# Cached values of seven batches spread over eight pairs, the eighth beside the output projection; prompt scores in split q and k

## The chip, the cores and the metric

One NeuronCore of a Trainium2 chip runs the whole program. The metric is the device time in microseconds (us) of one execution. Before the change it is 1991.42 us, the median of three runs (1989.58 to 1993.14).

## What is computed

A two-layer decoder step for a prompt group (one sequence of 1024 tokens) and a sample group (eight sequences of four new tokens, each with 4096 cached positions in 32 pages of 128). The first layer is a pooling mixer, the second "forgetting attention" with 16 heads of width 64. Only the second layer and its output projection matter here:

```python
def fox_attend(q, cq, qpos, k, ck, kpos, v):     # prompt and sample alike
    s = einsum('bqhd,bkhd->bhqk', q, k) * scale
    s = s + cq[..., :, None] - ck[:, None, :]     # forget values, cumulated
    s = where(kpos <= qpos, s, -inf)
    return einsum('bhqk,bkhd->bqhd', softmax(s), v)

y = (o * silu(z)) @ w_out                         # both groups
x = x + y;  y_out = rms_norm(x, final_norm)
```

For the sample group, k and v are the pages that a page table names, followed by the four new rows. All pages of the cached values are 134 MB in float32.

## The kernel before, in words

The attention phase comes after the projection phase. The sample scores (q times cached k) have already been computed there and lie in DRAM as `s_scr`. What is left runs as a loop over eight **pairs** (`pair(b)`, one on each engine). Pair `b` does two things at once: the whole prompt attention of heads 2b and 2b+1, and the softmax and values of sample batch `b` (all 16 heads).

A pair has eight **slots**, one for each block of 128 prompt queries, in the order `QBLOCKS = (0, 7, 1, 6, 2, 5, 3, 4)`. Slot `s` needs scores against 128 to 1024 keys for two heads. TensorE (PE) computes them in plain float32 (`scores`, line 1519: `qa` and `ka`, 66 rows, two of them for the forget values; a float32 matmul shows as two records) into `ps_a` and `ps_c`. VectorE (DVE) takes the maximum (`prompt_max`, L1800), ScalarE (ACT) the exponential (`prompt_exp`, L1702), DVE multiplies by the reciprocal of the sum (`prompt_norm`, L1805 and L1808), PE transposes (`prompt_turn`, L1547), ACT copies out (`prompt_evac`, L1709), and PE multiplies with the values in the next slot (`prompt_values`, L1560). DVE then gates the result (`gate`, L1869).

Between these steps PE takes cached value pages of the sample batch (`sample_pages`, L1592; eight records for a page). `V_FIRST` spreads the 32 pages of a batch over the slots as 2, 6, 2, 6, 3, 5, 4, 4. For every eight pages (an octet `o`) there is one `sample_scores(b + 1, o)` on DVE (L1826, L1830, for the following batch), one `sample_exp` on ACT (L1717), one `sample_turn` on PE (L1572) and one `sample_evac` on ACT (L1727). `new_scores`, `common_max`, `new_turn`, `sample_last`, `sum_exp` and `sample_out` come once for each batch.

Every engine runs its instructions in the written order. SyncE (SP) issues the loads in the order of the pages: `v_page(b, p)` waits until the page that was in one of the ring's `VR = 8` places has been used, then loads 512 KB. Into that stream are written the loads of the next pair's q and k rows (`qk_rows`), its prompt values (`v_pair`), and two `score_half` (each 512 KB of `s_in` and twice 256 KB of `d_sb`, the decay terms) for each batch. A load written late therefore waits behind the pages ahead of it.

Before pair 0, DVE does all four `sample_scores(0, o)`, `new_scores(0)` and `common_max(0)`; pair 0's `prompt_max` stands behind them.

After pair 7 comes the output projection over eight row tiles (L1665 to L1667): z and w_out are split into a high and a low part in `float32r` (ACT makes the high part, L1747 and L1751; DVE subtracts for the low part, L1893 and L1899), and each product is three passes (high·high, high·low, low·high). The sample rows are projected in between, and each tile is normalised and stored. The same three-pass form is used in all projections (L812 to L814).

Of the kernel before, what the change touches and what calls it, by code (L numbers as in the profile page):

```python
# [26 lines left out]
P = 128  # L27
# [89 lines left out]
def build(nc, x_prompt, x_sample, state_pool, cache_k, cache_v, cache_logf, page_table, norm_g,  # L117
# [17 lines left out]
    with ExitStack() as ctx:  # L135
# [130 lines left out]
        ka = [place(f"ka{i}", [AUG, 2, SEQ], F32, big_at(at_qk[i] + 2048)) for i in range(2)]  # L266
        v_pr = [place(f"v_pr{i}", [P, TT, P], F32, big_at((AT_F + 4096, 15168)[i])) for i in range(2)]
# [6 lines left out]
        wo_at = [big_at(n) for n in (9024, 10048, 0, 1024, 4160, 5184, 6208, 7232)]  # L274
# [5 lines left out]
        fn_b = place("fn_b", [P, DM], F32, big_at(AT_K + 2048))  # L280
# [58 lines left out]
        ld_v_first, ld_qk_first = sem("ld_v_first"), sem("ld_qk_first")  # L339
# [21 lines left out]
        def v_pair(eng, b):  # L361

            eng.dma_start(v_pr[b % 2][:, :, :], v_prompt[0, 0].rearrange("(t p) h d -> p t (h d)", p=P)
                          [:, :, P * b:P * b + P]).then_inc(ld_v[b % 2] if b else ld_v_first, 16)

        def qk_rows(eng, b, i):
# [3 lines left out]
                .then_inc(ld_qk[b % 2] if b else ld_qk_first, 16)  # L370
# [996 lines left out]
        T2 = [("s", 0)]  # L1367
        for s_ in range(SLOTS):
            T2 += [(h_, s_, f_) for h_ in range(2) for f_ in range(len(fills(s_, h_)))]
            if s_ in (1, 3, 5):  # L1370
                T2.append(("s", (s_ + 1) // 2))
            if s_ == 5:
                T2.append(("n",))

        def t2_name(key):
            return "z" if key[0] == "s" else "x" if key[0] == "n" else fills(key[1], key[0])[key[2]][2]
# [4 lines left out]
        def t2_at(b, key):  # L1381

            return b * len(T2) + T2.index(key)

        def t2_free(b, key):

            i = b * len(T2) + T2.index(key)
            same = [j for j in range(i) if t2_name(T2[j % len(T2)]) == t2_name(key)]
# [3 lines left out]
        V_FIRST = (0, 2, 8, 10, 16, 19, 24, 28, 32)  # L1392
        W_ORDER = (4, 5, 6, 7, 0, 1, 2, 3)

        w_full = [sem(f"w_full{k}") for k in range(KT8)]
        ld_os, ld_fn, st_o, st_y, o_free = (sem(n) for n in ("ld_os", "ld_fn", "st_o", "st_y", "o_free"))
# [9 lines left out]

        act_wh, dve_wl, act_zh, dve_zl = (sem(n) for n in ("act_wh", "dve_wl", "act_zh", "dve_zl"))
# [3 lines left out]
        def sync_attend(sp):  # L1411
# [14 lines left out]
            def next_pair(b, p):  # L1426

                if p == VR + 2 and b < NB - 1:
                    sp.wait_ge(pe_s, 16 * b) if b else sp.wait_ge(pe_qk, UNITS)
                    qk_rows(sp, b + 1, 0)  # L1430
                if p == VR + 5 and b < NB - 1:
                    qk_rows(sp, b + 1, 1)
                if p == VR + 8 and b < NB - 1:
                    past(sp, pe_pvp, SLOTS * b)
                    v_pair(sp, b + 1)
# [7 lines left out]
            for b in range(NB - 1):  # L1443
                for p in range(VR, PAGES):
                    v_page(b + 1, p)
                    next_pair(b, p)
                for p in range(VR):
                    v_page(b + 2, p)
            for k in range(4, KT8):
                w_out_rows(k)  # L1450
            for p in range(VR, PAGES):
                v_page(NB, p)
                if p == 15:
                    sp.wait_ge(pe_s, 16 * (NB - 1))
                    for k in range(4):
                        w_out_rows(k)
            sp.wait_ge(st_y, 16 * (TT + 1))

        def gpsimd_attend(pool):
# [32 lines left out]
            pool.wait_ge(pe_pv, VR + PAGES * NB)  # L1492
# [14 lines left out]
        def tensor_attend(pe):  # L1507
# [16 lines left out]
            def new_scores(b):  # L1524
# [3 lines left out]
                if b:  # L1528
                    pe.wait_ge(act_t2, t2_at(b - 1, (1, 6, 0)) + 1)
# [497 lines left out]
```

## Time and profile before

| what | us |
|---|---|
| median of three runs | 1991.42 |
| profiled execution, its time | 1999.29 |
| profiled execution, its span | 1997.6 |
| attention, pairs 0 to 7 (1353 to 1887) | 534 |
| of it pair 0, from its first score (1353 to 1444) | 91 |
| output projection and end (1887 to 1998) | 111 |

In the page, PE is busy for 92% of the span and the DMA engines carry 207 GB/s on average. How to read the stages: the window view gives busy time, instruction count, the clock granted to TensorE (as a share of 2.4 GHz), the mean busy share of the 16 DMA engines, and GB/s, for each stretch. The timeline gives the start of each group of instructions and, in brackets, the engine's idle time before it and what ended that.

### The profile page before, as it was taken

What the parts mean: (1) busy time and instruction counts of PE and PEld (TensorE: products, weight loads), DVE (VectorE), ACT (ScalarE), POOL (GpSimd) and SP (SyncE); (2) the same over time, 40 slices, a digit from 0 to 9 for tenths busy, and PEclk for the clock granted to TensorE, in tenths of its full rate; (3) what the DMA queues carried; (4) which work ended last, traced back from release to release, by engine and by line L of the source; (5) the groups of instructions that cost most, each with busy time, mean ns of one, the idle gap of its engine ahead of it and who ended that gap; (6) DMA issues with size and microseconds to landing.
All of it is one profiled execution on the core that took longest, in us unless ns stands there. A gap on an engine that the chain in (4) does not pass through costs nothing.

```text
span 1997.6 us, 37941 instructions
## 1 busy us (share of the span) xinstructions
PE 1837.1 (92%) x15120; PEld 1362.1 (68%) x15120; DVE 1124.7 (56%) x1810; ACT 547.3 (27%) x1241; POOL 296.4 (15%) x328
## 2 busy tenths in 40 slices
PE   4999999999999989899989999885999998999997
PEld 3877887787788767677778777773545554555676
DVE  5434544474465367877776777663545554554533
ACT  5121121121111143111112111212444444454521
POOL 0000000000000003444444444330000000000100
PEclk9999999999999989899999999996899999999999
DMA  5111111111112156899999999989999899999721
GB/s 139 38 45 53 43 45 42 48 43 49 43 48 64 32 177 231 286 339 313 319 319 351 321 323 308 329 296 333 336 330 305 301 333 327 311 327 344 271 85 56
DMA packets 228677, 414.49 MB, mean 207 GB/s; under 512 B 17553, under 2 KB 137010, under 8 KB 228238
## 3 DMA queue, kind: packets, MB, share of 16 engines
q1 hardware_dynamic: 168364, 252.17, 38.0%
q0 software_dynamic: 42160, 150.54, 21.2%
q10 hardware_dynamic: 17986, 9.42, 1.7%
q8 instruction: 121, 1.98, 0.4%
q14 instruction: 46, 0.38, 0.1%
HBM read 370.85 MB, written 41.94 MB: 207 GB/s over the span
## 4 chain that ended last, share of the span: by engine, by line
PE 52%; DMA 22%; DVE 13%; SPq 5%; issue 4%; POOL 2%; ACT 2%; POOLq 0%; DVEq 0%; ACTq 0%
DMA k_raw<-in_cache_k_dram,k_idx 16%; PE ps_a L812 5%; PE ps_a L814 4%; PE ps_a L813 4%; DVE kt L1293 4%; PE ps_b L812 3%; PE ps_b L814 3%; PE ps_b L813 3%; PE ps_c L812 3%; DMA d_sb<-decay 3%; PE ps_b L1592 3%; PE ps_c L814 3%; PE ps_c L813 3%; SPq L359 3%; PE ps_b L1560 2%
## 5 line engine op out<-in xcount | busy, mean ns | idle before, releaser
L1293 DVE STREAM_TRANSPOSE kt<-k_raw 128x1024 f32<-128x1024 f32 x256 | 309.9, 1232 | 145.7 <-DMA k_raw<-in_cache_k_dram,k_idx 140.6
L353 POOL DMA_INDIRECT k_raw<-in_cache_k_dram,k_idx x256 | 256.3, 1001 | 449.2 <-DVE kt L1293 291.0
L812 PE MATMUL ps_a<-h_hi,w_hi 128*128 128x512 f32 x656 | 263.2, 401 | 3.2 <-DVE w_lo L1115 3.2
L814 PE MATMUL ps_a<-h_hi,w_lo 128*128 128x512 f32 x656 | 256.4, 391 | 0.0
L813 PE MATMUL ps_a<-h_lo,w_hi 128*128 128x512 f32 x656 | 256.4, 391 | 0.0
L1115 DVE TENSOR_TENSOR w_lo<-w_raw,w_hi 128x1024 fp32r<-128x1024 f32 x97 | 109.1, 1125 | 163.1 <-ACT w_hi L642 160.4
L1592 PE MATMUL ps_b<-v_pg,pt_s 128*16 128x256 f32 x2048 | 147.4, 400 | 17.2 <-DMA v_pg<-in_cache_v_dram 16.1
L812 PE MATMUL ps_b<-h_hi,w_hi 128*128 128x512 f32 x384 | 154.2, 401 | 2.7 <-DVE w_lo L1115 2.7
L812 PEld LDWEIGHTS ps_a<-h_hi,w_hi 128*128 128x128 f32 x656 | 123.5, 188 | 39.1 <-issue 10.8
L814 PE MATMUL ps_b<-h_hi,w_lo 128*128 128x512 f32 x384 | 150.0, 391 | 0.0
L813 PE MATMUL ps_b<-h_lo,w_hi 128*128 128x512 f32 x384 | 149.7, 390 | 0.0
L954 PE MATMUL ps_c<-kt,q_bd 128*32 128x128 f32 x4096 | 136.4, 290 | 11.0 <-DVE kt L1293 9.8
L814 PEld LDWEIGHTS ps_a<-h_hi,w_lo 128*128 128x128 f32 x656 | 123.5, 188 | 26.6
L813 PEld LDWEIGHTS ps_a<-h_lo,w_hi 128*128 128x128 f32 x656 | 123.8, 189 | 23.8
L954 PEld LDWEIGHTS ps_c<-kt,q_bd 128*32 128x32 f32 x4096 | 117.5, 117 | 26.6 <-issue 23.3
L1800 DVE TENSOR_REDUCE pp_nm<-ps_a 128x1 f32<-128x128 f32 (+3 forms) x64 | 48.4, 756 | 151.5 <-PE ps_a L1521 151.3
L1173 DVE TENSOR_TENSOR x_p<-x_p,ps_c 128x512 f32<-128x512 f32 x128 | 87.6, 687 | 78.0 <-PE ps_c L814 78.0
L642 ACT CAST w_hi<-w_raw 128x1024 fp32r<-128x1024 f32 x97 | 96.0, 989 | 120.0 <-PE ps_c L814 86.3
L812 PE MATMUL ps_c<-w_hi,y_hi 128*128 128x512 f32 x256 | 103.9, 406 | 2.8 <-DVE x_p L1173 2.7
L814 PE MATMUL ps_c<-w_hi,y_lo 128*128 128x512 f32 x256 | 101.7, 397 | 0.0
L813 PE MATMUL ps_c<-w_lo,y_hi 128*128 128x512 f32 x256 | 101.7, 397 | 0.0
L1709 ACT COPY pt_p<-b 128x384 f32<-128x384 f32 (+3 forms) x168 | 73.6, 468 | 97.8 <-PE b L1547 96.1
(284 smaller groups left out, 2854.5 us busy)
## 6 DMA issues: line engine op xcount, KB each, us to landing
v_pg<-in_cache_v_dram SPq DMA_DIRECT2D x256, 512.0 KB, 7.6
w_raw<-in_w_in_pool_dram SPq DMA_DIRECT2D x32, 512.0 KB
w_raw<-in_w_in_attn_dram SPq DMA_DIRECT2D x32, 512.0 KB
w_raw<-in_w_out_pool_dram SPq DMA_DIRECT2D x16, 512.0 KB
s_scr<-ss_st ACTq DMA_DIRECT2D x64, 128.0 KB, 6.2
s_in<-s_scr SPq DMA_DIRECT2D x16, 512.0 KB, 7.4
d_sb<-decay SPq DMA_DIRECT2D x32, 256.0 KB, 8.5
z_scr<-x_st SPq DMA_DIRECT2D x8, 528.0 KB, 5.0
```

The costliest lines, as they stand in the source:

```text
L353: pool.indirect_dma_start(k_raw[:, k, :], None, cache_rows, bass.IndirectOffsetOnAxis(ap=k_idx[:, u, k:k + 1], axis=0)).then_inc(k_full[k] ...
L359: return sp.dma_start(v_pg[:, p % VR, :], cache_v[0, bass.ds(page, 1)].rearrange("o k h d -> (o k) (h d)"))
L642: nc.scalar.copy(w_hi[slot][:, 0:width], raw[:, 0:width]).then_inc(act_hi, 1)
L812: nc.tensor.matmul(ps, ah, bh, start=j == 0, stop=False)
L813: nc.tensor.matmul(ps, ah, bl, start=False, stop=False)
L814: mm = nc.tensor.matmul(ps, al, bh, start=False, stop=j == last)
L954: mm = nc.tensor.matmul(b5[32 * cg:32 * cg + 32, PAGE * hh:PAGE * hh + PAGE], q_bd[:, i, :], kt[s % 2][:, i, :], start=j == 0, stop=j == 3 ...
L1115: V.tensor_tensor(w_lo[slot][:, 0:width], raw[:, 0:width], w_hi[slot][:, 0:width].bitcast(F32), ALU.subtract).then_inc(dve_lo, 1)
L1173: V.tensor_tensor(x_p[:, u, half], x_p[:, u, half], out_b[u % 2][:, :], ALU.add).then_inc(dve_o, 1)
L1293: V.transpose(kt[u % 2][:, :, 32 * k:32 * k + 32], k_raw[:, k, :].rearrange("p (i c) -> p i c", c=32)).then_inc(dve_kt, 1)
L1592: mm = nc.tensor.matmul(ps_b[32 * j:32 * j + 16, 0:256], pt_s[:, p % 4, block:block + 4, :].rearrange("p c q -> p (c q)"), v_pg[:, p % VR, ...
L1709: nc.scalar.copy(pt_p[:, h, first:first + n, :].rearrange("p t q -> p (t q)"), t2_bank((h, s, f))[:, 0:P * n]).then_inc(act_t2, 1)
```

## The change

It has two parts.

**The values.** The 32 groups of two slots (eight pairs times four) are numbered by `g`; those with `g % 8 == 0`, which are slots 0 and 1 of pairs 0, 2, 4 and 6, get no cached pages, and the other 28 take the 28 octets of batches 0 to 6 in order (`OCTET`). So batches no longer begin and end with pairs. In a group the eight pages are split as before (`V_SPLIT`: 2+6, 2+6, 3+5, 4+4). `sample_turn`, `sample_exp` and `sample_evac` of an octet, and the once-a-batch steps, move to the slots where the octets now are. Batch 7 (`NT`) is turned and multiplied in the output projection, one octet before tile 0 and one after each of tiles 0, 1 and 2; its transposes go to another bank. The sample rows' own projection moves by two tiles (from after tiles 2, 3, 5 to after 4, 5, 6). Of w_out, one row block instead of four is split ahead of the end of pair 7; four blocks are loaded after the last scores, since their place is now used by `qk_hi`. Pair 0's scores no longer stand behind the four sample scores of batch 0: two are done in slot 0, two in slot 1 (behind the `gate` of slot 0).

**The prompt scores.** For pairs 1 to 7 ACT casts q and k to a high part (`high_qk`: 4 of 5 pieces in slot 7 of the pair before, between the two `prompt_evac`, the fifth in slot 0), DVE subtracts for the low part (`low_qk`, same slots, after `prompt_norm`), and the scores are three `float32r` passes. Pair 0 keeps float32.

```diff
+        OCTET = {g_: next(octets) for g_ in range(4 * NB) if g_ % 8}
+        V_SPLIT = (2, 2, 3, 4)
+        QK_PARTS = ((0, 0, P), (1, 0, P), (1, P, SEQ), (0, 7 * P, SEQ), (0, P, 7 * P))
+        QK_AT = (2, 4, 5)
@@ sync_attend
+            for n in range(VR, NB * PAGES):
+                v_page(n // PAGES + 1, n % PAGES)
+                for q in range(NB):
+                    next_pair(q, n - FIRST_PAGE[q])
+                next_batch(n // PAGES, n % PAGES)
@@ tensor_attend, scores
+                if b and s < 3:
+                    pe.wait_ge(dve_qk, 5 * (b - 1) + QK_AT[s])
-                            nc.tensor.matmul(ps_h[h][:, c:end], qa[b % 2][:, h, P * qb:P * qb + P],
-                                             ka[b % 2][:, h, c - first:end - first], start=True, stop=end < last)
+                            nc.tensor.matmul(ps_h[h][:, c:end], q_hi[:, h, q], k_hi[:, h, k], start=True, stop=False)
+                            nc.tensor.matmul(ps_h[h][:, c:end], q_hi[:, h, q], k_lo[:, h, k], start=False, stop=False)
+                            nc.tensor.matmul(ps_h[h][:, c:end], q_lo[:, h, q], k_hi[:, h, k],
+                                             start=False, stop=end < last)
@@ tensor_attend, pair
-                    if s in (1, 3, 5):
-                        sample_turn(b, (s + 1) // 2)
+                    if after and after[1]:
+                        sample_turn(*after)
                     if s < SLOTS - 1:
                         scores(b, s + 1)
                     elif b < NB - 1:
                         scores(b + 1, 0)
@@ tensor_attend, output projection, tile i
+                    sample_turn(NT, 0)
+                    octet_pages(NT, 0, 0, 8)
+                if i < 3:
+                    sample_turn(NT, i + 1)
 ...
                 mm.then_inc(pe_y, 1)
+                if i < 3:
+                    octet_pages(NT, i + 1, 0, 8)
@@ scalar_attend
+            def high_qk(b, first, last):
+                for i, (j, c, end) in enumerate(QK_PARTS[first:last]):
+                    if first + i == 0:
+                        act.wait_ge(pe_s, 16 * b)
+                        act.wait_ge(ld_qk[b % 2], 32 * ((b + 1) // 2))
+                    nc.scalar.copy(qk_hi[j][:, :, c:end], (qa, ka)[j][b % 2][:, :, c:end]).then_inc(act_qk, 1)
@@ scalar_attend, pair
                     prompt_evac(b, s, 0)
-                    if s in (1, 3, 5):
-                        sample_exp(b, (s + 1) // 2)
+                    if s == 7 and b < NB - 1:
+                        high_qk(b + 1, 0, 4)
+                    if s == 0 and b:
+                        high_qk(b, 4, 5)
+                    if after and after[1]:
+                        sample_exp(*after)
                     prompt_evac(b, s, 1)
@@ scalar_attend, after the pairs
+            high_w(1)
+            sample_exp(NT, 0)
+            high_w(2)
+            high_w(3)
+            sample_evac(NT, 0)
+            sample_exp(NT, 1)
@@ vector_attend, pair
                     prompt_norm(b, s, 0)
                     prompt_norm(b, s, 1)
+                    if s == 7 and b < NB - 1:
+                        low_qk(b + 1, 0, 4)
+                    if s == 0 and b:
+                        low_qk(b, 4, 5)
+                    if (b, s) == (0, 0):
+                        sample_scores(0, 0)
+                        sample_scores(0, 1)
@@ vector_attend, before the pairs
             queries(0)
-            for o in range(4):
-                sample_scores(0, o)
-            new_scores(0)
-            common_max(0)
```

## Rows read from the trace of the kernel before

**Rows 1.** The page: busy shares, then the DMA engines' share in 40 slices.
```profile
PE 1837.1 (92%) x15120; PEld 1362.1 (68%) x15120; DVE 1124.7 (56%) x1810; ACT 547.3 (27%) x1241; POOL 296.4 (15%) x328
...
DMA  5111111111112156899999999989999899999721
```

**Rows 2.** Windows: pairs 0, 3 and 7, then the end; span, busy (count), clock, DMA, GB/s.
```profile
1353.00:1444.00 91.00, 67.69 (x569) 35.84 (x568) 38.91 (x98) 31.44 (x84) 1.03 (x1) 0.76 0.97 339
...
1572.00:1637.00 65.00, 59.31 (x585) 33.71 (x582) 33.10 (x83) 30.33 (x82) 2.25 (x4) 0.95 0.91 317
...
1828.00:1887.00 59.00, 57.54 (x586) 33.73 (x580) 32.62 (x69) 37.09 (x92) 4.63 (x8) 1.00 0.91 341
1887.00:1998.00 111.00, 99.27 (x476) 76.04 (x472) 41.83 (x62) 21.99 (x38) 10.39 (x19) 0.96 0.20 71
```

**Rows 3.** Waits of 1400 to 1885: who waited for what, total us, times, longest.
```profile
DVE s_sb L1826 <- DMA d_sb<-decay: 27.2, 6, 5.6
```

**Rows 4.** Windows of 3 us in the middle of pair 3, columns as in Rows 2.
```profile
1611.00:1614.00 3.00, 1.60 (x22) 0.77 (x20) 1.07 (x3) 0.00 (x0) 0.00 (x0) 1.00 1.02 411
1614.00:1617.00 3.00, 1.25 (x16) 0.26 (x16) 2.92 (x7) 1.21 (x3) 0.00 (x0) 0.87 1.03 402
1617.00:1620.00 3.00, 2.27 (x14) 1.29 (x14) 1.42 (x4) 1.79 (x5) 0.00 (x0) 0.50 1.05 402
```

**Rows 5.** DVE and PE timelines of pair 3: the wait, the pages around it at both clocks.
```profile
1612.90 0.88 DVE L1826 SCALAR_TENSOR_TENSOR s_sb<-s_in,cq,d_sb 128x256 f32<-128x256 f32 x2 [5.63 <-DMA d_sb<-decay]
...
1617.72 1.54 PE L1547 MATMUL b<-con,p_p 128*128 128x128 f32 x6 [1.70 <-DVE p_p L1808]
1619.19 1.06 PE L1592 MATMUL ps_b<-v_pg,pt_s 128*16 128x256 f32 x8
...
1626.96 1.49 PE L1592 MATMUL ps_b<-v_pg,pt_s 128*16 128x256 f32 x24
```

**Rows 6.** PE timeline: float32 scores of 128 and 1024 keys, the border of pairs 3 and 4.
```profile
1637.75 0.61 PE L1608 MATMUL ps_b<-st_l,lsel 128*128 128x1 f32 x4
1638.21 0.47 PE L1519 MATMUL ps_a<-ka,qa 66*128 66x128 f32 x2
...
1642.89 1.98 PE L1519 MATMUL ps_a<-ka,qa 66*128 66x512 f32 x4
1644.71 0.22 PE L1521 MATMUL ps_a<-caus_b,ident_b 128*128 128x128 bf16 x1
```

**Rows 7.** PE timeline of the output projection: float32r passes of 512 columns.
```profile
1900.04 0.39 PE L1667 MATMUL b<-wo_hi,z_lo 128*128 128x512 f32 x1
1900.27 0.39 PE L1665 MATMUL ps_c<-wo_hi,z_hi 128*128 128x512 f32 x1
```

**Rows 8.** Groups by form, 1200 to 1998: busy, mean ns of one, idle before.
```profile
L1709 ACT COPY pt_p<-b 128x256 f32<-128x256 f32 x32 | 12.0, 376 | 24.1 <-PE b L1547 23.7
...
L1893 DVE TENSOR_TENSOR z_lo<-z_t,z_hi 128x1024 fp32r<-128x1024 f32 x8 | 9.8, 1219 | 0.0
...
L1747 ACT CAST z_hi<-z_t 128x1024 fp32r<-128x1024 f32 x8 | 8.3, 1039 | 0.0
```

**Rows 9.** Timelines of the start: DVE and SP.
```profile
1361.37 0.88 DVE L1826 SCALAR_TENSOR_TENSOR s_sb<-s_in,cq,d_sb 128x256 f32<-128x256 f32 x2 [11.86 <-DMA d_sb<-decay]
...
1371.84 0.33 SPq L535 DMA_DIRECT2D z_t<-z_scr  x1
...
1383.64 0.75 DVE L1808 TENSOR_SCALAR p_p<-p_p,pp_r 128x1024 f32<-128x1024 f32 x1
```

**Rows 10.** Chain of waits, 1340 to 1440: start, length, what.
```profile
1380.37 17.40 DMA v_pg<-in_cache_v_dram
```

**Rows 11.** DVE timeline: the step that closes each pair's common maximum.
```profile
1443.46 0.21 DVE L1861 STREAM_TRANSPOSE st_nm<-mx_b 128x32 f32<-128x32 f32 x1
...
1827.32 0.21 DVE L1861 STREAM_TRANSPOSE st_nm<-mx_b 128x32 f32<-128x32 f32 x1
```

**Rows 12.** Loads by line: KB of one, median us from issue to landing.
```profile
z_t<-z_scr SPq DMA_DIRECT2D x1, 528.0 KB, 3.7
```

More of the change, by code:

```diff
@@ L1364, in fills @@
             return [(0, 3, "y"), (3, min(4, n - 3), "x")] + ([(7, 1, "z")] if n == 8 else [])
[L1367 to L1373, printed above, removed]
-        def t2_name(key):
-            return "z" if key[0] == "s" else "x" if key[0] == "n" else fills(key[1], key[0])[key[2]][2]
+        NT = NB - 1
@@ new lines, in build, with octet, next_octet, opened @@
+        octets = iter((b_, o_) for b_ in range(NT) for o_ in range(4))
+        OCTET = {g_: next(octets) for g_ in range(4 * NB) if g_ % 8}
+        FIRST_PAGE = [8 * sum(g_ < 4 * p_ for g_ in OCTET) for p_ in range(NB)]
+        V_SPLIT = (2, 2, 3, 4)
+        def octet(p, s):
+            return OCTET.get(4 * p + s // 2)
+        def next_octet(p, s):
+            return OCTET.get(4 * p + (s + 1) // 2) if s % 2 else None
+        def opened(p, s):
+            if s % 2 == 0:
+                return None
+            oc = octet(p, s)
+            return 0 if (p, s) == (0, 1) else oc[0] + 1 if oc and oc[1] == 3 else None
@@ new lines, in build @@
+        T2 = []
+        for p_ in range(NB):
+            for s_ in range(SLOTS):
+                oc_, nx_ = octet(p_, s_), next_octet(p_, s_)
+                if s_ % 2 == 0 and oc_ and oc_[1] == 0:
+                    T2.append(("s",) + oc_)
+                T2 += [(p_, h_, s_, f_) for h_ in range(2) for f_ in range(len(fills(s_, h_)))]
+                if nx_ and nx_[1]:
+                    T2.append(("s",) + nx_)
+                    if nx_[1] == 3:
+                        T2.append(("n", nx_[0]))
@@ L1617, in pair @@
                         prompt_values(b - 1, SLOTS - 1)
-                    if s == 0:
-                        sample_turn(b, 0)
-                    if s == 7 and b < NB - 1:
-                        new_scores(b + 1)
+                    now, after, fresh = octet(b, s), next_octet(b, s), opened(b, s)
+                    if s % 2 == 0 and now and now[1] == 0:
+                        sample_turn(*now)
+                    if fresh is not None:
+                        new_scores(fresh, b, s)
                     if s:
@@ L1636, in pair @@
                         scores(b + 1, 0)
[L1637 to L1638 removed]
+                    if after and after[1] == 3:
+                        new_turn(after[0])
             pe.sem_inc(pe_pv, VR)
@@ L1902, in pair @@
             def pair(b):
-                more = b < NB - 1
                 for s in range(SLOTS):
+                    now, fresh = octet(b, s), opened(b, s)
                     prompt_max(b, s, 0)
```

273 lines of the change are left out of this document (156 added, 117 removed).

## The prediction

> **What bounds the kernel now.** I read the page first: PE is busy 92% of the span, and the DMA engines are near 90% in the last third but for the end [rows 1]. Then the windows by pair and the end [rows 2]: in pair 3 PE is busy 59.3 of 65 us and DMA 0.91 of the time; in the output projection PE is busy nearly throughout and DMA 0.20. So the pairs use two resources almost fully and the end only one. Then the waits: DVE waits for `d_sb` 27.2 us in six waits [rows 3]. The windows of pair 3 show it at work [rows 4]: DMA share over 1.0 at 402 to 411 GB/s, PE busy 1.60 and 1.25 of 3 us, and after that a granted clock of 0.50 (1.2 GHz). DVE stood 5.63 us in front of `sample_scores`, PE's transpose waited for it, and eight records of a page took 1.06 us against 1.49 us for 24 a little later [rows 5]. I put the loss at about 7 us in a pair: 4 us idle and 3 us at the lower clock. Pair 7, which has no such wait, takes 59 us [rows 2]. The pairs' closing steps lie 383.9 us apart over six pairs, 64.0 each [rows 11].
>
> **PE work that goes from the pairs.** Three pages are 24 records in 1.42 us from start to start, 0.473 us a page [rows 5], so the 32 pages of a batch cost 15.1 us; four sample turns of 0.6 us and the last step of about 1.1 us make it 18.8 us. Spread over eight pairs it is 2.4 us each, and all of it returns in the end phase: the total work of PE does not fall by this.
>
> **The scores.** 1024 keys in float32 take 1.82 us from start to start, and the row's 1.98 us hold a tail of 0.16; 128 keys, 0.47 us with that tail, take 0.31 [rows 6]. The other six sizes read from the timeline in this way are 0.44, 0.65, 0.86, 1.08, 1.29 and 1.51; the eight add up to 7.96, for two heads 15.9 us a pair. A float32r pass of 512 columns takes 0.23 us from start to start [rows 7], so 512 keys cost 0.69 us. A short pass is bound by its weight load: four matmuls of one column with 128-column weights take 0.46 us, 0.115 us each [rows 6], and a whole 128-key float32 matmul 0.31 us in two records, 0.15 each. I take 0.13 us for passes of 128 and 256 columns, 0.175 for 384, 0.23 for 512. Per head: 0.40 (128), 0.40, 0.53, 0.69, 0.93, 1.09, 1.21, 1.37 (1024) = 6.6 us, 13.2 us a pair: 2.7 us saved. With short passes at 0.19 it is 1.0 us saved, with pure streaming 3.8 us. Over seven pairs: 19 us of PE work, between 7 and 27.
>
> The Trainium skill (TensorE: Matmul & The Clock Gate, Wait — 56ns, not 53.3ns?) gives N/2.4 GHz plus 2.5 ns for every warm pass: 216 ns for 512 columns, where this trace has 230, and 109 for 256, for which the trace has no float32r row. By it a pair's scores would cost 11.7 us and 4.2 us would be saved, 10 us more in all than by the rows.
>
> **The cost on ACT and DVE at the border.** A cast of 1024 elements takes 1.04 us on ACT, the subtraction 1.22 us on DVE, a copy of 256 elements 0.38 us [rows 8]. The four pieces in slot 7 (256, 256, 1792, 256 elements) are 2.8 us on ACT and 3.3 us on DVE; the fifth (1536) 1.5 and 1.75. The engines' sums have room (DVE 33 and ACT 30 of 65 us [rows 2]), but both run in order. In slot 7 ACT's second `prompt_evac` stands behind 2.8 us of casts, so `prompt_values` of slot 7 comes late; DVE's first `prompt_max` of the next pair stands behind the subtractions, some 2 us late; in slot 0 the fifth piece holds DVE until about 2 us after the 1024-key scores of slot 1 are ready. Where an octet's `sample_exp` also stands in slot 7 (borders to pairs 1, 3 and 5), PE's `sample_turn`, written ahead of the next scores, waits some 4 us for ACT. Laid out step by step from the old border (scores of slot 7 to scores of slot 2, 1630.0 to 1653.5, 23.5 us): about 27 us where octets remain, about 22 us into pairs 2, 4 and 6, though these lose eight pages (3.8 us) there. So the border costs roughly 3 to 5 us of PE idling a pair, and eats the scores' gain and more.
>
> **DMA.** A page is 0.524 MB at about 400 GB/s [rows 4], 1.3 us. Pair 3 has 0.91 of 65 = 59 us of DMA work; four pages less leave 54 us. The demand falls below PE's time, so the backlog behind which `d_sb` lands shrinks. It needn't vanish: the two `score_half` stand at the same places in the page stream. I keep 2 of the 7 us.
>
> **Pairs.** Stall-free old pair 58; minus 2.4 (values), minus 2.7 (scores), plus 3 to 5 (border), plus 2 (stall that stays): 59.5 on average for pairs 1 to 6, about 62 for odd and 57 for even ones, against 64.0: 27 us saved. Between 55 each, the DMA work (54 saved), and 65 each, where border and lower clock cost all that is saved (6 lost). Pair 7 had no `d_sb` wait and had the w_out casts; it now gets the sample scores of batch 7: plus 1, between minus 4 and plus 3.
>
> **Pair 0.** Now DVE waits until 1361.4 for the first `d_sb` and slot 1's probabilities are normalised at 1383.6 [rows 9]; afterwards a page load takes 17.4 us, since seven blocks of z (128 x 1056 float32 each, 3.8 MB) come in beside it [rows 10]. After the change the maximum of slot 1 doesn't stand behind all of that, but `gate` of slot 0 still waits for z, whose load is issued at 1371.8 [rows 9] and takes 3.7 us [rows 12]. So slot 1 comes only some 3 us earlier. But there are no pages in slots 0 and 1, and the first eight lie ready when slot 2 starts: of the page waits and the low clock (0.76 over pair 0 [rows 2]) I expect 9 us to go. In all 12 saved, between 6 and 16.
>
> **The end.** PE is the bound there, busy at full clock until its last matmul, so the 18.8 us of batch 7 come in full. In front of tile 0 PE waits for ACT: one cast of w_out (1.04), `sample_exp` (1.3), two casts more, then `sample_evac`: 3 us idle in sum, and 1 us more if the late blocks of w_out are late. A tile (48 passes of 0.23 = 11 us) plus the pages and the turn make 15.2 us; 4.2 MB of pages and 1 MB of rows take 13.1 us at 400 GB/s, so the ring refills just in time. The moved sample projection costs nothing: it is the same work on PE, still one tile ahead of the end; if its cover is gone, about 2 us. In all plus 23, between 19 and 35.
>
> **Sum.** Minus 12, minus 27, plus 1, plus 23 = minus 15 us. The profiled execution (time 1999.3, span 1997.6) would become 1984.3. Its time lies 7.9 us above the median of the runs; on the median 1991.4 − 15 = 1976.
>
> **Rivals.** *DMA only*: the border hides behind the DMA work, pairs fall to 55 to 56 us. For: shares above 1.0 in the middle of the pairs [rows 4]. Against: PE itself is busy 59 of 65 us [rows 2]. −54 −4 −14 +23 = about −47: 1944. *Cheap passes*: the short passes cost only their columns; for it speak the 0.115 us spacing of weight loads [rows 6]; minus 8 to 10 more: 1967. *Border and clock* (slower): PE idles 3 to 4 us in slot 1 of the pairs without pages and 4 us at the borders to 1, 3 and 5, and each time the clock falls to 1.2 GHz, as after the idling in pair 3 [rows 4, 5]; then pairs cost 65 us: −10 +6 +3 +23 = +22, 2013. It decides once pairs 1 to 6 take over 62 us on average (64.0 less (23 + 1 − 12)/6 = 2.0). Of this clock rule the Trainium skill (TensorE: Matmul & The Clock Gate, HAM oscillation — how this bites in real kernels) says that gaps in the matmul stream bring the slow clock back, again and again in a loop; the trace agrees for pair 3. *Late pages in the end*: the octets 1 to 3 land behind the row loads and stores, 4 to 5 us each: minus 15 + 14 = −1, 1990.
>
> **How the numbers follow.** Forecast 0.42, *cheap passes* 0.10, *DMA only* 0.16, *border and clock* 0.17, *late pages* 0.15. A measurement of this kernel tells 0.2% (4 us) from no change. Faster: 0.40 + 0.10 + 0.16 + 0.01 + 0.03 = 0.70. Within 0.2%: 0.02 + 0.03 + 0.07 = 0.12. Slower: 0.13 + 0.05 = 0.18. The range goes from the price of *DMA only*, with half of that case (0.08) left out below it, to 2003, with two thirds of *border and clock* (0.11) left out above: 1944 to 2003.
>
> **What would show it.** Pair 0 some 79 us instead of 91, pairs 57 to 62 with odd ones longer, the waits of DVE for `d_sb` down to a third, DMA share about 0.9 still; new waits of PE for ACT and DVE in slots 7, 0 and 1; the passes of 256 columns 0.13 us apart; from the end of pair 7 to the end 134 us. Wrong it is if the pairs go to 55 (the border hidden), or if the clock in slots 7 to 1 is 0.50 in most pairs.

## The result

The changed kernel is slower: 2055.01 us, the median of four runs (2037.42 to 2065.51), against 1992.28 us for the kernel before in the same session, a ratio of 1.0306 with a 95% interval of 1.0225 to 1.0387. The prediction said 1976.

The profiled execution of the changed kernel has a span of 2046.3 us. Its page, the busy shares first, then the granted clock and the DMA share in 40 slices:

```profile
PE 1859.5 (91%) x15288; PEld 1417.3 (69%) x15288; DVE 1156.2 (56%) x1845; ACT 574.3 (28%) x1276; POOL 296.6 (14%) x328
...
PEclk9999999999999999999999999879987977888899
DMA  5111111111111257998999999989868867688851
```

PE is *busy* 22 us longer than before [rows 1], although its work was to fall. The clock row tells why: in the pairs, slices 28 to 38, it reads 7 or 8 in eight of eleven. And the DMA row, at 8 and 9 up to slice 37 before [rows 1], falls to 6 in slices 30, 33 and 35.

To see where the time went I cut both traces at the first `prompt_max` of each pair and at the first pass of tile 0. The windows of the changed kernel, pair 0 to pair 7 and then the end (columns as in rows 2):

```profile
1350.00:1430.00 80.00, 56.84 (x486) 33.69 (x485) 38.84 (x90) 33.65 (x86) 1.03 (x1) 0.83 0.95 330
1430.00:1494.00 64.00, 58.17 (x627) 39.33 (x626) 37.44 (x90) 32.65 (x80) 2.47 (x4) 0.95 0.89 310
1494.00:1560.00 66.00, 54.71 (x523) 37.54 (x522) 35.85 (x85) 34.48 (x88) 2.35 (x4) 0.87 0.71 237
1560.00:1627.00 67.00, 62.08 (x624) 40.66 (x623) 37.77 (x90) 32.86 (x83) 2.36 (x4) 0.88 0.90 309
1627.00:1701.00 74.00, 61.57 (x518) 42.55 (x519) 35.74 (x84) 33.81 (x87) 2.25 (x4) 0.76 0.66 219
1701.00:1773.00 72.00, 63.89 (x620) 41.43 (x621) 37.65 (x89) 32.79 (x83) 2.33 (x4) 0.86 0.82 284
1773.00:1847.00 74.00, 62.69 (x553) 43.27 (x550) 36.60 (x89) 33.82 (x87) 0.00 (x0) 0.78 0.69 238
1847.00:1920.00 73.00, 65.34 (x667) 40.14 (x666) 45.02 (x93) 41.24 (x98) 6.67 (x12) 0.87 0.86 318
1920.00:2046.00 126.00, 114.52 (x678) 83.71 (x676) 38.62 (x60) 24.10 (x51) 10.40 (x19) 0.95 0.44 162
```

Set against the prediction's terms, in profiled time (spans 1997.6 and 2046.3, a difference of 48.7):

| stage | before | after | difference | predicted |
|---|---|---|---|---|
| attention starts (first mask pass) | 1353.7 | 1349.7 | −4 | 0 |
| pair 0, to the start of pair 1 | 92.9 | 80.5 | −12 | −12 |
| pairs 1 to 6 | 383.9 | 416.3 | +32 | −27 |
| pair 7 and the end | 167.1 | 199.8 | +33 | +24 |

Pair 0 came out as forecast (the earlier start lies ahead of everything that the change touches; the kernels below start between 1342 and 1356). The end is 9 us off. The prediction went wrong in pairs 1 to 6, by 59 us: 69.4 us each instead of 59.5. Yet the wait that it expected to shrink to a third did just that, from 27.2 us [rows 3] to 7.4. The waits of the changed kernel, 1440 to 1910 (who, for what, total us, times, longest):

```profile
PE b L1593 <- DVE p_p L1901: 20.4, 22, 2.5
DVE q_lo L1993 <- ACT q_hi L1823: 19.6, 12, 1.9
...
PE ps_b L1650 <- DMA v_pg<-in_cache_v_dram: 13.9, 10, 3.6
...
DVE s_sb L1919 <- DMA d_sb<-decay: 7.4, 3, 4.1
...
PE b L1618 <- ACT s_sb L1785: 7.3, 4, 3.0
```

The first of them is not new. In the kernel before, over 1440 to 1885, it was:

```profile
PE b L1547 <- DVE p_p L1808: 18.7, 34, 1.7
```

It has become rarer but longer. The waits for pages were there too, but none was longer than 1.5 us (11.0 us in all in pairs 1 to 6); those for `s_sb` are new. All are short, at most 3.6 us on PE. What they do is seen in windows of 4 us at the border of pairs 3 and 4 and in the first half of pair 4:

```profile
1620.00:1624.00 4.00, 3.43 (x39) 2.13 (x30) 1.61 (x5) 2.72 (x5) 0.00 (x0) 1.00 0.96 370
1624.00:1628.00 4.00, 1.65 (x24) 1.30 (x22) 3.54 (x9) 1.98 (x8) 0.00 (x0) 0.97 1.04 406
1628.00:1632.00 4.00, 4.00 (x11) 2.79 (x12) 2.16 (x3) 1.80 (x3) 0.00 (x0) 0.50 0.70 282
1632.00:1636.00 4.00, 2.87 (x10) 1.54 (x9) 2.63 (x5) 1.67 (x3) 0.00 (x0) 0.50 0.00 0
1636.00:1640.00 4.00, 3.39 (x16) 3.27 (x16) 1.48 (x3) 2.71 (x7) 0.00 (x0) 0.50 0.00 0
1640.00:1644.00 4.00, 2.93 (x14) 2.39 (x12) 0.42 (x1) 2.09 (x7) 0.00 (x0) 0.50 0.01 4
1644.00:1648.00 4.00, 4.00 (x37) 3.43 (x40) 0.67 (x3) 0.84 (x4) 0.00 (x0) 0.50 0.00 0
1648.00:1652.00 4.00, 4.00 (x34) 2.81 (x26) 3.72 (x11) 0.65 (x2) 0.00 (x0) 0.97 0.43 105
...
1668.00:1672.00 4.00, 1.51 (x18) 0.77 (x14) 2.21 (x9) 1.03 (x4) 0.00 (x0) 1.00 1.04 254
1672.00:1676.00 4.00, 1.68 (x11) 0.88 (x12) 0.00 (x0) 0.00 (x0) 0.00 (x0) 0.52 0.84 292
1676.00:1680.00 4.00, 4.00 (x25) 2.00 (x25) 0.17 (x2) 1.95 (x6) 0.00 (x0) 0.50 0.99 364
```

PE is busy 1.65 of 4 us at the border, and then the granted clock is 0.50 (1.2 GHz) for 20 us. In the slots without pages the eight places of the ring are full and the DMA engines stand still for 16 us (0.00 to 0.01). At 1668 the pages that are to make up for it come late, PE is busy 1.51 and 1.68 of 4 us, and the clock falls once more. It is not this border alone: over the first 15 us of each of the pairs 2 to 7 the mean clock is 0.50 to 0.57, in pair 1 it is 0.84. The prediction named a clock of 0.50 in slots 7 to 1 of most pairs as a sign of being wrong; over the whole of these slots it is 0.64 to 0.74 from pair 2 on. Two causes, then, each possible alone: the casts at the border, and the slots without pages. The first runs take the change apart along this line.

### The profile page after: what moved, and what is told of

Its sections match the earlier page's. It is cut to its first block, busy times and chain, and to the rows that moved or that the text cites. A ratio compares the mean times of both kernels' runs of the same rounds, so it can differ in the third digit from the quotient of the medians.

```text
span 2046.3 us, 38323 instructions
## 1 busy us (share of the span) xinstructions
PE 1859.5 (91%) x15288; PEld 1417.3 (69%) x15288; DVE 1156.2 (56%) x1845; ACT 574.3 (28%) x1276; POOL 296.6 (14%) x328
## 4 chain that ended last, share of the span: by engine, by line
PE 52%; DMA 22%; DVE 13%; issue 5%; SPq 4%; ACT 2%; POOL 2%; POOLq 0%; ACTq 0%; DVEq 0%
DMA k_raw<-in_cache_k_dram,k_idx 15%; DVE kt L1296 5%; PE ps_a L815 5%; PE ps_a L817 4%; PE ps_a L816 4%; PE ps_b L1650 4%; DMA v_pg<-in_cache_v_dram 4%; PE ps_b L815 3%; PE ps_b L817 3%; PE ps_b L816 3%; PE ps_c L815 3%; PE b L1593 3%; PE ps_b L1606 3%; PE ps_c L816 3%; PE ps_c L817 3%
## 5 line engine op out<-in xcount | busy, mean ns | idle before, releaser
L815 PEld LDWEIGHTS ps_a<-h_hi,w_hi 128*128 128x128 f32 x656 | 123.9, 189 | 39.6 <-issue 10.3
L1593 PE MATMUL b<-con,p_p 128*128 128x128 f32 x480 | 87.0, 314 | 37.3 <-DVE p_p L1901 29.2
L1593 PEld LDWEIGHTS b<-con,p_p 128*128 128x128 f32 x480 | 61.5, 157 | 70.9 <-DVE p_p L1901 54.3
L1650 PEld LDWEIGHTS ps_b<-v_pg,pt_s 128*16 128x16 f32 x2048 | 49.0, 99 | 83.8 <-issue 34.9
```

What stands on the lines that cost most here:

```text
L815: nc.tensor.matmul(ps, ah, bh, start=j == 0, stop=False)
L1593: mm = nc.tensor.transpose(t2_bank((b, h, s, f))[:, P * i:P * i + P], p_p[:, h, c:c + P], ident)
L1650: mm = nc.tensor.matmul(ps_b[32 * j:32 * j + 16, 0:256], pt_s[:, p % 4, block:block + 4, :].rearrange("p c q -> p (c q)"), v_pg[:, p % VR, ...
```

## The experiments

The table gives all of them; times are medians of 4 to 10 executions, a ratio is against the kernel before on the same chip. The last four columns come from the one profiled execution, cut as above: the time of pairs 1 to 6, what PE is idle in them (the small matmuls added in after_warm count as busy), the mean clock in them, and pair 7 with the end.

| kernel | us | ratio (95% interval) | pairs 1 to 6 | PE idle | clock | pair 7 and end |
|---|---|---|---|---|---|---|
| before | 1992.28 | 1 | 383.9 | 30.9 | 0.96 | 167.1 |
| changed | 2055.01 | 1.0306 (1.0225 to 1.0387) | 416.3 | 53.9 | 0.84 | 199.8 |
| values_only | 2018.36 | 1.0120 (1.0092 to 1.0147) | 390.7 | 42.2 | 0.93 | 194.6 |
| split_only | 2034.51 | 1.0212 (1.0175 to 1.0248) | 416.7 | 42.0 | 0.86 | 169.6 |
| no_casts | 2008.27 | 1.0082 (1.0055 to 1.0108) | 380.2 | 41.9 | 0.91 | 192.6 |
| after_warm | 2029.44 | 1.0169 (1.0118 to 1.0221) | 402.7 | 36.9 | 0.95 | 196.7 |
| casts_last | 2047.95 | 1.0286 (1.0246 to 1.0326) | 407.8 | 57.0 | 0.87 | 200.0 |
| values_spread | 2013.26 | 1.0106 (1.0062 to 1.0151) | 388.7 | 42.8 | 0.95 | 195.5 |
| values_gap_mid | 2013.37 | 1.0125 (1.0088 to 1.0162) | 380.6 | 42.2 | 0.97 | 194.3 |
| shift_one | 1973.53 | 0.9918 (0.9884 to 0.9952) | 358.9 | 19.9 | 1.00 | 182.1 |
| before_early | 1991.79 | 1.0008 (0.9980 to 1.0036) | 380.6 | 27.0 | 0.96 | 167.1 |
| values_early | 2022.13 | 1.0130 (1.0085 to 1.0176) | 403.5 | 45.0 | 0.91 | 192.1 |
| after_early | 2053.95 | 1.0288 (1.0236 to 1.0340) | 419.5 | 51.4 | 0.84 | 196.2 |
| shift_split | 2013.63 | 1.0119 (1.0086 to 1.0152) | 388.4 | 39.6 | 0.92 | 184.3 |

### One half of the change at a time

**values_only** keeps the spread batches and puts float32 scores back; **split_only** is the kernel before with the split scores (and the places in memory and the order of w_out that they need):

```diff
 values_only, against the changed kernel
-                            if b == 0:
+                            if True:
                                 nc.tensor.matmul(ps_h[h][:, c:end], qa[b % 2][:, h, q], ka[b % 2][:, h, k],
-                    if s == 7 and b < NB - 1:
-                        high_qk(b + 1, 0, 4)
-                    if s == 0 and b:
-                        high_qk(b, 4, 5)
```

> The changed kernel with float32 scores in every pair: no casts of q and k on ScalarE and no subtractions on VectorE; the values stay spread, the eighth batch stays in the output projection. Theory BORDER (the casts stand in front of work that TensorE waits for, and the idling lowers the clock): most of the loss goes, 1985 to 2005 us. Theory GAP (slots 0 and 1 of pairs 2, 4 and 6 have no pages, TensorE idles there and DMA with it): it stays at 2035 to 2055 us, and the granted clock of these pairs stays below 0.85.

> The kernel before with the split scores alone: pages as before (2, 6, 2, 6, 3, 5, 4, 4 in each pair), casts and subtractions in the same slots as in the change. w_out is split in the order of its blocks, and its last four blocks are loaded after the last scores, as in the change. Theory BORDER: slower than before, pairs 68 us and more, 2015 to 2040 us. Theory GAP: pages fill the wait, pairs 62 to 64 us, 1980 to 1995 us.

split_only came out in the range of BORDER; values_only, at 2018, in neither range, since each theory had only one cause. Measured against the kernel before: +25 us for the values, +41 us for the scores, +63 for both. The halves add up within 4 us, so each costs something by itself. But they don't cost it in the same place: in pairs 1 to 6 the values lose 7 us and the split 33; of the values' loss the larger part is pair 7 with the end, 27.5 us longer, where 24 were forecast. Nor in the same way: both add 11 us of idling, but the split takes the clock from 0.96 to 0.86, which is some 116 us of 417 at 1.2 GHz against 27 of 384 before (worked out from the mean clock), the values only to 0.93. In split_only, whose order of the pages is that of before, all six pairs take 69 to 71 us. PE's timeline at the border of its pairs 1 and 2 shows one of the waits, for ACT, whose `sample_exp` stands behind the casts:

```profile
1507.45 1.11 PE L1589 MATMUL b<-con,s_sb 128*128 128x128 f32 x4 [1.53 <-ACT s_sb L1734]
```

### The passes without their casts, and the clock

**no_casts** runs three float32r passes on the uncast q and k and leaves out the casts and the subtractions, so the three passes add up to three times the scores; it shows only the time. **after_warm** is the changed kernel with small bf16 matmuls on PE in front of the turns at which it waits: 20 in front of `prompt_values` and 20 more in front of the turn of slot 0, 30 to 60 in slot 1, 50 in front of the sample turn in slot 7. **casts_last** moves `high_qk` behind the rest of the slot's work on ACT.

```diff
 no_casts, against the changed kernel
-                            (q_lo, k_lo), (q_hi, k_hi) = qk_lo[b % 2], qk_hi
+                            q_hi = q_lo = qa[b % 2][:, h, q].bitcast(F32R)
+                            k_hi = k_lo = ka[b % 2][:, h, k].bitcast(F32R)
 ...
 after_warm, against the changed kernel
+            def warm(n, bank):
+                for _ in range(n):
+                    nc.tensor.matmul(bank, ident_b[:, :], caus_b[:, :], start=True, stop=True)
 ...
+                    if b and s == 0:
+                        warm(20, ps_a[:, 512:640])
 ...
 casts_last, against the changed kernel
-                    if s == 7 and b < NB - 1:
-                        high_qk(b + 1, 0, 4)
                     if after and after[1]:
                         sample_exp(*after)
                     prompt_evac(b, s, 1)
                     if after and after[1]:
                         sample_evac(*after)
+                    if s == 7 and b < NB - 1:
+                        high_qk(b + 1, 0, 4)
```

> The changed kernel with three float32r passes, but without casts and subtractions: all three passes read the unsplit q and k, so the scores of pairs 1 to 7 are three times too large; this is left out on purpose. Only the work of ScalarE and VectorE at the border is gone, the passes of TensorE are the same. BORDER: 1970 to 1995 us. GAP: 2025 to 2050 us, since TensorE has even less to do in the slots without pages.

> The changed kernel with additional bf16 matmuls of 128 columns (0.06 us each at full clock) whose result nobody uses, in the places where TensorE waits at the borders: 20 ahead of the values of slot 7 and of the first transposes of slot 0, 30 or 60 in slot 1, 50 ahead of the sample turn in slot 7. No wait is taken away. If the lower clock carries the loss: pairs 2, 4 and 6 granted 0.95 and more, 2000 to 2020 us. If the waits themselves carry it: 2045 to 2070 us with the clock up or not.

> The changed kernel with ScalarE's casts of q and k behind both copies of the transposed probabilities and behind the exponentials and the copy of the sample octet, instead of between them. Nothing is taken away. Theory BORDER as an order effect: the values of slot 7 and the sample turn don't wait, but the next scores wait 1.5 to 2 us; 2030 to 2045 us against 2055. If the sum of ScalarE's and VectorE's work at the border counts and not its order: 2050 to 2060 us.

All three came out between the ranges of their two theories: neither the casts nor the clock carries the whole loss. Without the casts the changed kernel takes 47 us less (2055 − 2008). Against values_only, which differs from it in the form of the scores alone, the passes save 10 us, not 19 (the two intervals overlap a little). The dummies, which add work to PE, take 26 us off: so at least four tenths of the 63 us that the change costs are lost through the lower clock (the dummies can't keep it up everywhere: pair 6 stays at 0.90). Moving the casts behind the other work of ACT changes nothing that is clear of noise: 7 us less, with intervals that lie within each other for the most part. They still lie ahead of the next scores, and PE now waits there for DVE's low part of k, 9.3 us in six waits. The windows of pair 4, in after_warm and in no_casts, against 0.76 in the changed kernel:

```profile
1627.00:1694.00 67.00, 59.42 (x660) 42.82 (x657) 36.41 (x87) 34.13 (x88) 2.26 (x4) 0.95 0.75 245
```
```profile
1607.00:1676.00 69.00, 59.64 (x545) 41.03 (x543) 31.54 (x80) 30.46 (x83) 2.25 (x4) 0.83 0.72 246
```

In no_casts pair 4 still has a clock of 0.83 and 69 us, with no casts at all. That loss comes from the values' part of the change.

### Where the slots without pages stand

Three kernels on values_only. **values_spread** keeps four pages of the octet ahead of a gap back and takes them in slots 0 and 1; **values_gap_mid** puts the gaps of pairs 2, 4 and 6 into slots 4 and 5; **shift_one** has a single gap, slots 0 and 1 of pair 0, so that every pair has 32 pages again (24 in pair 0), and only the last octet of batch 7 is left for the output projection (w_out is split as in the kernel before).

```diff
 values_gap_mid, against values_only
-        OCTET = {g_: next(octets) for g_ in range(4 * NB) if g_ % 8}
+        OCTET = {g_: next(octets) for g_ in range(4 * NB) if g_ not in (0, 10, 18, 26)}
 values_spread, against values_only
+                if oc is None:
+                    if q == 0:
+                        return
+                    oc = octet(q - 1, SLOTS - 1)
+                    start, n = (5, 3) if s % 2 else (4, 1)
 ...
 shift_one, against values_only
-        octets = iter((b_, o_) for b_ in range(NT) for o_ in range(4))
-        OCTET = {g_: next(octets) for g_ in range(4 * NB) if g_ % 8}
+        octets = iter((b_, o_) for b_ in range(NB) for o_ in range(4))
+        OCTET = {g_: next(octets) for g_ in range(4 * NB) if g_}
```

> The kernel with the values alone moved (float32 scores), but of the octet ahead of each group without pages four pages are kept back and taken in that group: 2 and 2 instead of 4 and 4 in slots 6 and 7, then 1 in slot 0 and 3 in slot 1. The number of pages of each batch and the loads' order stay. Theory GAP (no work for TensorE in slots 0 and 1 of pairs 2, 4 and 6, and a full ring that stops DMA there): pairs 1 to 6 take 360 to 372 us instead of 391 (before: 384), the time is 1990 to 2002. If the gap is harmless and the pairs are bound otherwise (chain of the softmax steps, DMA in the other slots): 2012 to 2022.

> The values alone, with the groups without pages in slots 4 and 5 of pairs 2, 4 and 6 instead of slots 0 and 1 (pair 0 as before). Slots 4 and 5 have 384 and 768 keys, and before the change the loads ran late there. Theory GAP with the 1024-key slot as its place: better than 2018, 2003 to 2012, since the wait for a 1024-key softmax is filled again. If only the stop of DMA counts: 2015 to 2022, as there is a gap of the same size.

> Float32 scores, and every octet of all eight batches moved by one group only: pair 0 starts without pages, no other pair has a gap, and one octet instead of four is left for the output projection. w_out is split as before the change. It keeps the start (19 us less up to the first score of pair 1) and leaves out the gaps and three quarters of the batch in the end. Expected from the stages: minus 19, pairs 1 to 6 as before the change, end plus 5 for the octet, plus 1 for its last step, plus 2 to 5 of waiting: 1978 to 1988 us. If the gain at the start is only borrowed (DMA late in pair 1): 1992 to 2000 us.

The intervals of values_spread and values_gap_mid overlap with that of values_only. So GAP, as it was written down, fails: with pages in slots 0 and 1 the pairs should have fallen to 360 to 372 us, and they took 388.7. PE's wait for the probabilities did shrink, from 18.5 us in values_only to 12.7, but its wait for pages grew from 12.6 to 17.8, and the idle time is the same. What the three kernels share is that the DMA engines rest: in pairs 2, 4 and 6 of values_only for 16, 14 and 17 us, of values_spread for 10, 8 and 11, of values_gap_mid for 11, 9 and 12 (stretches of 1 us with a share under 0.2; in the pairs of shift_one it is 1). In values_gap_mid two of the pairs with a gap take 58.7 and 58.9 us, and the pairs right behind them 70.9 and 66.3. The loss wanders, it does not go; values_gap_mid's 2013 us lie between its two ranges. shift_one beats both kernels: 1973.5 us, 17 us less than the kernel before in the same session, and less than the 1978 to 1988 expected, for its pairs 1 to 6 take 25 us less than before where they were expected unchanged. Three windows out of its pairs, and its only waits for pages between 1428 and 1848:

```profile
1489.00:1549.00 60.00, 56.71 (x585) 32.96 (x585) 33.01 (x85) 30.67 (x84) 2.30 (x4) 1.00 0.97 345
1549.00:1608.00 59.00, 55.82 (x579) 32.49 (x580) 32.39 (x82) 29.67 (x81) 2.29 (x4) 1.00 0.97 348
1608.00:1668.00 60.00, 56.76 (x588) 33.16 (x585) 32.94 (x84) 30.67 (x85) 2.29 (x4) 1.00 0.98 345
...
PEld ps_b L1650 <- DMA v_pg<-in_cache_v_dram: 2.5, 4, 0.7
PE ps_b L1650 <- DMA v_pg<-in_cache_v_dram: 0.3, 2, 0.2
```

59.6 to 60.2 us a pair, clock 1.00, DMA 0.97: with the same 32 pages as the pairs of before, which take 64.0. The longest idle of PE in a pair of shift_one is 1.02 us. Compare slot 1 and the middle of pair 4 in values_only with slot 1 of pair 2 in shift_one:

```profile
1625.32 1.09 PE L1593 MATMUL b<-con,p_p 128*128 128x128 f32 x8 [2.00 <-DVE p_p L1897]
...
1629.24 0.63 PE L1618 MATMUL b<-con,s_sb 128*128 128x128 f32 x4 [1.66 <-ACT pt_p L1777]
...
1660.81 0.62 PE L1650 MATMUL ps_b<-v_pg,pt_s 128*16 128x256 f32 x8 [3.37 <-DMA v_pg<-in_cache_v_dram]
```
```profile
1497.76 1.48 PE L1650 MATMUL ps_b<-v_pg,pt_s 128*16 128x256 f32 x24
1500.26 1.09 PE L1593 MATMUL b<-con,p_p 128*128 128x128 f32 x8 [1.02 <-DVE p_p L1884]
```

In shift_one three pages (1.48 us) cover most of the time that DVE takes for the probabilities of slot 1. In values_only there are none, and PE waits 2.00 us, and again 1.66 us for ACT.

### Is it the load of the second score half?

The wait for `d_sb` is all but gone from shift_one (0.2 us). **before_early**, **values_early** and **after_early** take the three kernels as they are and write the load of the second score half ahead of the next pair's q, k and v instead of behind them. **shift_split** adds the split scores to shift_one.

```diff
-                if p == VR + 11 and 0 < b < NB - 1:
+                if p == VR and 0 < b < NB - 1:
                     sp.wait_ge(dve_s, b * N_S + 4)
                     score_half(sp, b + 1, 1)
```

> The kernel before with one number changed: the load of the second half of the sample scores (s_in and d_sb) is written ahead of the next pair's q, k and v instead of behind them, eleven pages earlier. Theory LOADS (the 4.4 us a pair that the kernel with pages shifted by one group has over the kernel before come from this half being written right behind 1.5 MB of pair loads): DVE's waits for d_sb fall from 27 us to under 5, pairs 1 to 6 take about 60 us each instead of 64.0, the clock in them is 0.98 or more; 4 x 6 = 24 us less, 1967 us. Theory LIGHTER (the shifted kernel is faster because its pair 0 has lost two slots of pages and the last octet is in the projection, and the pairs are set by the load rate): the wait moves to the pages, pairs stay at 63 to 64 us, 1987 to 1993.

> The change's values part alone (prompt scores in float32), with the same earlier load of the second score half. LOADS (the spread batches lose because the pair loads, at a place in the page stream that moves from pair to pair, collide with the score halves): the pairs that take 64 to 70 us fall towards 60, at least 15 us less than the values part alone (2018): 2003 or below. Theory GAP (what counts is that TensorE and the loads stand in the slots without pages and the next group waits for pages): 2013 to 2020, unchanged within 5 us, with d_sb waits (only 6.3 us there) gone.

> The whole changed kernel with the same earlier load. Its waits for d_sb are 7.4 us in three waits. LOADS: 10 to 15 us less than the changed kernel, about 2042. GAP and BORDER: no more than the few us of d_sb, 2048 to 2057.

> The kernel with pages shifted by one group (float32 scores, 1973.5 us, pairs 59.6, clock 1.00, DMA share 0.97), with the prompt scores in split q and k added as in the change. Theory BORDER (the casts make TensorE idle 3 to 4 us at each border and the clock falls there, whatever the pages do): about +41 us as on the kernel before, +6 a pair, pairs 65 to 66 us, clock 0.88: about 2013. Rival GAP (the border costs only where it meets slots without pages): pairs stay within 1 us of 59.6, as the load rate sets them: 1972 to 1982.

LOADS falls, in all three kernels. In before_early the 27.2 us for `d_sb` [rows 3] are gone altogether from the waits, and the time is the same within 0.4%; LIGHTER had 1987 to 1993, and it is 1991.8. The wait moved to PE's pages (17.3 us in pairs 1 to 6, 11.0 before), and the pairs fell into two kinds. Pairs 1 to 6 of before_early by windows, then its wait for a page in pair 1, and two windows of 3 us in pair 4:

```profile
1443.00:1510.00 67.00, 60.86 (x586) 34.96 (x581) 32.94 (x84) 30.41 (x82) 2.38 (x4) 0.92 0.93 309
1510.00:1573.00 63.00, 57.31 (x596) 33.19 (x594) 33.60 (x85) 30.28 (x82) 2.26 (x4) 1.00 0.97 328
1573.00:1632.00 59.00, 56.13 (x574) 32.00 (x572) 32.41 (x83) 30.28 (x82) 2.26 (x4) 1.00 0.99 346
1632.00:1698.00 66.00, 61.62 (x598) 35.72 (x596) 33.70 (x85) 30.27 (x82) 2.25 (x4) 0.92 0.92 314
1698.00:1758.00 60.00, 57.11 (x591) 32.83 (x585) 33.40 (x85) 30.39 (x83) 2.27 (x4) 1.00 0.98 346
1758.00:1824.00 66.00, 60.92 (x584) 35.20 (x582) 32.88 (x84) 30.16 (x82) 2.25 (x4) 0.92 0.91 294
...
1474.01 1.05 PE L1592 MATMUL ps_b<-v_pg,pt_s 128*16 128x256 f32 x8 [3.89 <-DMA v_pg<-in_cache_v_dram]
...
1659.00:1662.00 3.00, 0.93 (x8) 0.16 (x8) 0.00 (x0) 0.89 (x3) 0.00 (x0) 0.84 0.98 326
1662.00:1665.00 3.00, 2.46 (x13) 1.40 (x14) 0.00 (x0) 0.32 (x1) 0.00 (x0) 0.50 1.06 379
```

Three pairs have a clock of 0.92 and take 65 to 67 us, two take 59 to 60 us at 1.00. What lies between is mostly one wait: in pair 4 it is 2.00 us long, PE is busy 0.93 of 3 us, and about ten us at 0.50 follow. Six us are paid for two. (Pair 2 is the third kind: a wait of 2.49 us, no fall of the clock, 62.5 us.) This also says what shift_one does right: its pairs are all of the cheap kind. The kernel before with an early load reaches it in two pairs out of six, with the same 32 pages, so neither their number nor, as LIGHTER had it, the rate of the loads holds a pair at 64 us; it is that no wait of PE grows long. Why the page stream of shift_one never makes a long wait and that of before_early in four pairs of six, these runs don't tell. In values_early the waits for pages are 44 us in all (1435 to 1906, PE and its weight loads), and the time is 2022 us against 2018, so there, too, it was not the score half. after_early, at 2054, is the changed kernel's time again.

shift_split costs 40 us over shift_one, as BORDER said (2013 expected, 2013.6 measured), with the pairs at 64.7 us on average. The border that the casts make needs no slot without pages to hurt. Its idle at the border to pair 5, in front of the turn that stands ahead of the scores:

```profile
1692.12 0.88 PE L1618 MATMUL b<-con,s_sb 128*128 128x128 f32 x4 [2.97 <-ACT s_sb L1780]
```

The same 2.97 us stand at the borders to pairs 3 and 5 of the changed kernel. ACT's `sample_exp` stands there behind 2.6 us of casts (1554.9 to 1557.4 in the changed kernel).

## Why the prediction was wrong

**Pair 0: right, for the reason given.** 93 to 80.5 us, against a forecast of 91 to 79.

**Pairs 1 to 6, the values' part: here two steps failed, together the largest miss.** With values_only the pairs take 65.1 us on average; the prediction's stall-free 58, less 2.4 for the values, plus 2 for the rest of the stall, make 57.6. That is 7.5 us in each of six pairs, 45 of the 59.

**The first of the two: "I keep 2 of the 7 us".** The `d_sb` waits fell as forecast, but I took the 7 us of a stalled pair as something that belongs to this wait and goes with it. before_early removes all of the wait and leaves pairs 1 to 6 at 380.6 us instead of 383.9, 63.4 a pair and not 58; its PE waits for pages instead. So 5.4 us of the stall stay, not 2: some 20 of the 45 us.

**The second: minus 2.4 us a pair for the values, true as work and not as time.** values_only is 1.7 us a pair above before_early and not 2.4 below it: the other 25 of the 45 us. (Both shares rest on one profiled execution of each kernel.) The pages that left a gap had covered DVE's normalising in slot 1, and the ring, full after eight pages, let the DMA engines rest for 16 us. Which of the two costs more is not shown; values_spread, which fills slots 0 and 1 again, gets back 2 of 391 us. I had the demand of loads as a mean over the pair (54 of 59 us). In the odd pairs it was never less: they still have 32 pages. In the even ones it was pressed into the other six slots. That the DMA engines would rest could be read from the code: eight places, and nothing to free them.

**The scores: right in kind, too large in size.** Passes of 256 columns are 0.12 us apart, against the forecast's 0.13, but the first pass of a head takes 0.20. PE's timeline of the changed kernel in pair 1:

```profile
1449.67 0.36 PE L1564 MATMUL ps_a<-k_hi,q_hi 66*128 66x256 f32 x1
1449.87 0.28 PE L1565 MATMUL ps_a<-k_lo,q_hi 66*128 66x256 f32 x1
1449.99 0.28 PE L1566 MATMUL ps_a<-k_hi,q_lo 66*128 66x256 f32 x1
```

The Trainium skill's N/2.4 GHz plus 2.5 ns (TensorE: Matmul & The Clock Gate, Wait — 56ns, not 53.3ns?) gives, as an estimate, 109 ns for 256 columns. The trace has 0.12 us for the later passes and 0.20 for the first one of a head, so that the rule is nearly met by all but the first.

Eight slots times two heads times 0.08 us are 1.3 us of the 2.7 us a pair; no_casts measures 10 us in all (10.5 over pairs 1 to 6, 1.8 a pair).

**The border: the idles were right, their price was not.** I had laid out some 4 us in front of `sample_turn` and 3 to 5 us of idling a pair; the trace shows 2.97 and the waits listed above. But the casts cost 36 us over pairs 1 to 6 (416.3 − 380.2), 6 us a pair, and the whole split 4.3 to 5.5 us a pair net (over six: 25.6 in the changed kernel against values_only, 32.8 in split_only, 29.5 in shift_split), where I had −2.7 + 4 = +1.3. In the changed kernel that is 3 us a pair more than forecast, 18 in six. What I left out, and this step failed too, was what follows an idle: some ten to twenty us at half the clock. I had it in *border and clock*, at 0.17, with 65 us a pair; it decides from an average of 62, and the pairs came to 69.4. The trace before had already shown the price: in rows 4 the clock is 0.50 after two windows of idling. The Trainium skill (TensorE: Matmul & The Clock Gate, HAM oscillation — how this bites in real kernels) describes gaps in the matmul stream that bring the slow clock back again and again. The changed kernel's trace agrees, with 0.50 to 0.57 at the start of each of the pairs 2 to 7: what the prediction held at 0.17 was the case that came.

**The end: +33 instead of +24.** The pages and turns of batch 7 came in full. In addition PE waits in front of tile 0, and tile 0 begins at 1.2 GHz (passes 0.43 us apart until 1924, then 0.23). PE's timeline of the changed kernel:

```profile
1910.41 4.47 PE L1650 MATMUL ps_b<-v_pg,pt_s 128*16 128x256 f32 x48 [1.71 <-ACT pt_s L1795]
1916.27 0.62 PE L1650 MATMUL ps_b<-v_pg,pt_s 128*16 128x256 f32 x8 [1.40 <-DMA v_pg<-in_cache_v_dram]
1918.60 1.05 PE L1650 MATMUL ps_b<-v_pg,pt_s 128*16 128x256 f32 x8 [1.70 <-DMA v_pg<-in_cache_v_dram]
...
1920.92 0.63 PE L1730 MATMUL ps_a<-wo_lo,z_hi 128*128 128x512 f32 x1
1921.35 0.63 PE L1731 MATMUL ps_a<-wo_hi,z_lo 128*128 128x512 f32 x1
```

The waits are 4.8 us, where the prediction had 3. The lower clock behind them makes the six pages of the first line take 1.5 us more than two groups of three at 2.4 GHz (1.49 us each) [rows 5], and tile 0's first nine passes 0.2 us more each: some 3 us, by this estimate, where the prediction had none. Another 2.5 us are the split in pair 7 (split_only). That is some 8 of the 9 us.

**Slips in the sums.** 58 − 2.4 − 2.7 + 4 + 2 is 58.9 us a pair and not 59.5. Against the terms themselves pairs 1 to 6 are 63 us too long, the 45 and the 18; against the 59.5 they are 59. The work of batch 7 adds up to 18.6 us and not 18.8, and *DMA only* to −49 and not −47. Nothing hangs on them.

**Still open.** Why the clock stays up after some of the waits: in shift_split the 2.97 us at the border to pair 3 left it at 1.00, the same wait at the other borders did not. And which place of the loads makes the page waits of values_only after a gap as long as they are: the earlier score half made its pairs 1 to 6 slower (403.5 against 390.7 in one profiled execution each), with the same time for the whole kernel within the intervals.

## What to carry to other kernels

When TensorE runs next to a load stream that is itself nearly full, price a new wait of a few us on TensorE at up to three times its length: the wait, and the half clock behind it. Removing the longest wait of another engine was worth nothing by itself here; ask which load would be the last one then, and undo that wait alone in a small kernel before a rebuild is planned on it. Work that is taken out of a slot must not be the work that covered another engine's step there, and a ring of loads should have something to fetch in every slot: one shift that keeps each pair the same (shift_one) gave 17 us, where spreading with gaps, and with a whole batch in the end phase, lost 25.

## What the runs showed of the hardware

Small matmuls put into TensorE's idle spots shortened the changed kernel by 26 us though they are pure extra work: pair 4 went from a clock of 0.76 and 74.8 us to 0.95 and 66.5 us.

Pairs of the same code take 59.7 us at a clock of 1.00 or 65 to 67 us at 0.92 (before_early), with one wait of 2 to 4 us between them. Idles of 1.02 us, the longest in the pairs of shift_one, leave the clock at 1.00. Between 2 and 3 us both happens: 2.00 us (before_early, pair 4) brought 0.50, while 2.49 us (before_early, pair 2) and 2.97 us (shift_split, border to pair 3) left 1.00.

In the changed kernel the first float32r pass of a head, behind another kind of matmul, takes 0.08 us longer than the ones behind it (0.20 against 0.12 us at 256 columns, 0.31 against 0.23 at 512).
